# A hybrid conv, pool and MoE layer: norm, router, shared expert and the experts' first weights in one stage with the projection

## The reference

```python
x = x + merged @ w_out                       # output projection and residual: res1
h = rms_norm(x, g_ffn)
scores = sigmoid(h @ w_router)               # 64 experts, 8 groups, best 4 groups, best 8 experts
gates = top_s / sum(top_s) * 2.5
x = x + sum_e gates_e * expert_e(h) + shared(h)      # SwiGLU, 256 wide each
ple_gate = sigmoid(rms_norm(x, g_ple) @ w_ple_gate)
x = x + ple_gate * (p @ w_ple)               # per-layer embedding, p is (1024, 256)
return rms_norm(x, g_final)
```

## Time and profile before

| | us |
|---|---|
| runs (3) | 2092.51, 2092.53, 2095.65; median 2092.53 |
| the profiled execution | 2092.55 |
| its span, first to last instruction | 2090.9 |
| busy: PE, DVE, ACT, POOL | 1855.5, 1378.5, 852.1, 851.6 |
| mean granted TensorE clock | 0.951 of full |

### The profile page before, as it was taken

How to read it: one execution, slowest core, us unless ns; L and a number is a source line. 1 busy time by engine, 2 the same in 40 slices (tenths; PEclk the granted TensorE clock), 3 DMA queues, 4 the chain that set the end, 5 groups by cost and what they waited for, 6 DMA issues and landing times. The chain is left out here.

```text
span 2090.9 us, 32643 instructions
## 1 busy us (share of the span) xinstructions
PE 1855.5 (89%) x8384; PEld 1493.8 (71%) x8385; DVE 1378.5 (66%) x1446; ACT 852.1 (41%) x1000; POOL 851.6 (41%) x688
## 2 busy tenths in 40 slices
PE   4999999988999677859999999999999999993594
PEld 2888888867888356647788778877787777882483
DVE  6299999347651556227666867766777767663766
ACT  4111110145100233246556666766666757561321
POOL 3457777546553220044343333433434434341330
PEclk9999999999999888979999999999999999996797
DMA  2211112212432322279999999999999999975402
GB/s 104 76 50 41 49 60 90 101 68 77 148 115 91 125 101 65 96 279 350 294 280 250 326 315 316 311 290 304 287 285 334 317 302 298 283 208 167 154 30 80
DMA packets 108850, 393.16 MB, mean 188 GB/s; under 512 B 18832, under 2 KB 21008, under 8 KB 100624
## 3 DMA queue, kind: packets, MB, share of 16 engines
q1 hardware_dynamic: 70656, 270.29, 34.9%
q0 software_dynamic: 28944, 88.90, 19.5%
q10 hardware_dynamic: 9216, 33.56, 4.2%
HBM read 329.22 MB, written 83.66 MB: 197 GB/s over the span
## 5 line engine op out<-in xcount | busy, mean ns | idle before, releaser
L168 PE MATMUL bank<-x_hi,w_hi 128*128 128x512 f32 x928 | 366.9, 395 | 26.0 <-DVE x_lo L232 15.9
L169 PE MATMUL bank<-x_lo,w_hi 128*128 128x512 f32 x928 | 364.1, 392 | 0.0
L170 PE MATMUL bank<-x_hi,w_lo 128*128 128x512 f32 x928 | 363.9, 392 | 0.0
L1499 DVE TENSOR_TENSOR gu_lo<-gu_raw,gu_hi 128x1024 fp32r<-128x1024 f32 x260 | 306.9, 1221 | 70.7 <-ACT gu_hi L1426 67.4
L1348 PE MATMUL bank<-gu_hi,xh 128*128 128x512 f32 x776 | 318.5, 410 | 13.6 <-DVE xl L1482 13.6
L1263 POOL DMA_INDIRECT acc_rows<-y,cur x98 | 185.0, 1888 | 352.7 <-ACT y L1422 338.2
L1350 PE MATMUL bank<-gu_lo,xh 128*128 128x512 f32 x776 | 305.7, 394 | 0.0
L1349 PE MATMUL bank<-gu_hi,xl 128*128 128x512 f32 x776 | 303.8, 392 | 0.0
L712 DVE SCALAR_TENSOR_TENSOR bank<-a_buf,c_w_dw,bank 128x1024 f32<-128x1024 f32 x232 | 276.8, 1280 | 0.0
L1426 ACT CAST gu_hi<-gu_raw 128x1024 fp32r<-128x1024 f32 x260 | 260.2, 1052 | 8.5 <-DMA gu_raw<-in_w_gu 8.5
L168 PEld LDWEIGHTS bank<-x_hi,w_hi 128*128 128x128 f32 x928 | 176.3, 190 | 67.7 <-issue 21.8
(11 more groups left out here) (272 smaller groups left out, 2913.3 us busy)
## 6 DMA issues: line engine op xcount, KB each, us to landing
gu_raw<-in_w_gu SPq DMA_DIRECT2D x260, 512.0 KB
dn_raw<-in_w_dn SPq DMA_DIRECT2D x64, 1024.0 KB
w_raw<-in_w_mix SPq DMA_DIRECT2D x56, 512.0 KB, 3.3
acc_in<-acc_rows ACTq DMA_DIRECT2D x16, 512.0 KB, 4.6
acc_rows<-zeros SPq DMA_DIRECT2D x10, 512.0 KB, 9.9
res<-in_x SPq DMA_DIRECT2D x8, 512.0 KB, 7.2
ga_d<-stage ACTq DMA_DIRECT2D x8, 512.0 KB, 2.6
gb_d<-stage ACTq DMA_DIRECT2D x8, 512.0 KB, 2.6
```

The source lines that it names most:

```text
L168: nc.tensor.matmul(o, wh[:, cols], x_hi[:, k, t], start=(i == 0), stop=False)
L169: nc.tensor.matmul(o, wh[:, cols], x_lo[:, k, t], start=False, stop=False)
L170: last = nc.tensor.matmul(o, wl[:, cols], x_hi[:, k, t], start=False, stop=(i == len(ks) - 1))
L1499: nc.vector.tensor_tensor(gl[s][:, w], rg[s][:, w], gh[s][:, w], ALU.subtract).then_inc(gu_split, 1)
```

## The change

Stages 2, 3 and 4 become part of the mixing stage's block; nothing separates them but semaphores.

- The router's weights are scaled by `g_ffn`, and the router product takes the unscaled `res1`. It has a 65th output: `pick` adds the squares of the residual to it, summed over partitions. A call of it (`logits`) stands behind each output chunk, two chunks late. The squares of tiles 0 to 6 are summed on POOL (`run_sq`), those of tile 7 stand by themselves (`part_sq`). The reciprocal root `inv8` is a value per token and is applied where something is evicted: to the logits, to the token rows (`store_rows`, in halves) and, spread to all partitions by a product with a diagonal (`inverse_to_all`), to the shared gate and up products.
- The four shared chunks follow the output chunks. Router, transposes, ranks and lists are called between their steps (`in_first_up`, `in_second_up`, `in_last_up`).
- The lists' one-hot tiles are made by 16 small DVE instructions per tile of tokens; ACT takes no part.
- The shared down products (`shared_down`) are split in their two input tiles; the flip of the first block of tokens stands behind the sixth. The first experts' weights are loaded once the last shared chunk is done. DVE alternates between the sums into `res1` and the low parts of the first expert's weights.
- `res1` goes channel-major to `res_d` and is read back in the last stage, where the rows' copy becomes an addition. Both accumulators start from zeros; 18 blocks are written beside chunks 3 to 11.
- The embedding product moves to the last stage, between the flips of the rows. Its result stays in SBUF.
- The priming scatters of the loop become three short writes to spare rows. Buffers of the loop have new places. The loop's instructions are the same.
- A clear of the semaphores and a barrier stand behind the experts.

The diff, cut to its core:

```diff
@@ sync, mixing stage
-            for n in range(2, END):
+            sp.wait_ge(blank, 1)
+            for n in range(2, ALL):
                 load_chunk(sp, n)
+                if 3 <= n < 3 + NT + 1:
+                    for a in range(2):
+                        sp.dma_start(acc_d[a][(n - 3) * P:(n - 2) * P, :], zeros[:]).then_inc(filled, 16)
...
+            for n in range(NT):
+                sp.wait_ge(evacuated, 2 * n + 2)
+                sp.dma_start(h2_d[n * P:(n + 1) * P, 0:D], rows[:, n % 2]).then_inc(row_out[n % 2], 16)
...
+            sp.wait_ge(done, ALL)
+            for e in range(2):
+                for p, w in enumerate(pieces):
+                    sp.dma_start(rg[e][:, w], i["w_gu"][e][:, w]).then_inc(gu_in[e][p], 16)
...
+            for k in range(KC):
+                sp.wait_ge(sd_read, k + 1)
+                sp.dma_start(res_d[k], res1[:, k, :]).then_inc(res_out[min(k, 2)], 16)
@@ tensor
+            def logits(k):
+                pe.wait_ge(out_read, k + 1)
...
+                for h in range(NH):
+                    t = slice(h * HALF, (h + 1) * HALF)
+                    nc.tensor.matmul(slots[2][0:E + 1, t], wr[:, k, :], res1[:, k, t], start=(k == 0), stop=False)
+            def inverse_to_all():
+                pe.wait_ge(diagonal, 1)
+                for h in range(NH):
+                    t = slice(h * HALF, (h + 1) * HALF)
+                    last = nc.tensor.matmul(slots[3][:, t], ones[:], dg.rearrange("p t e -> p (t e)")[:, t], start=True, stop=True)
+            def list_tokens(n):
+                pe.wait_ge(blocked, n + 1)
+                pe.wait_ge(numbered, n + 1)
...
+            def in_second_up(k):
+                if k == 1:
+                    inverse_to_all()
+                if k in (2, 3, 4):
+                    token_rows(2 * k - 4)
+                    token_rows(2 * k - 3)
+                if k == 5:
+                    ranks()
+                if k == 6:
+                    token_rows(6)
+                    token_rows(7)
+            def in_last_up(k):
+                if k % 2:
+                    list_tokens(k // 2)
...
+            chunk(OUT + 1, y_hi, y_lo)
-            pairs(OUT + 2, END, y_hi, y_lo, out_read, OUT)
+            for ch in range(2, KC):
+                chunk(OUT + ch, y_hi, y_lo)
+                logits(ch - 2)
+            logits(KC - 2)
+            pe.wait_ge(ran, KC - 2)
+            sum_of_squares(run_sq, False)
+            logits(KC - 1)
+            pe.wait_ge(squared2, KC)
+            sum_of_squares(part_sq, True).then_inc(lg_made, 1)
+            chunk(END, x_hi, x_lo, in_first_up)
+            chunk(END + 1, x_hi, x_lo, in_second_up)
+            chunk(END + 2, x_hi, x_lo)
+            chunk(END + 3, x_hi, x_lo, in_last_up)
+            list_tokens(4)
+            list_tokens(5)
+            shared_down(0, 0)
+            list_tokens(6)
+            list_tokens(7)
...
+            for n in range(KC):
+                if n:
+                    shared_down(n, 0)
+                shared_down(n, 1)
+                if n == 5:
+                    pe.wait_ge(gathered[0], 16)
+                    flip_rows(0)
@@ scalar
+            for k in range(KC):
+                act.wait_ge(out_read, k + 1)
+                if k >= 2:
+                    act.wait_ge(ran, k - 1)
+                nc.scalar.activation(part_sq[:] if k else run_sq[:], res1[:, k, :], ACT.Square).then_inc(squared2, 1)
+                nc.scalar.mul(x_hi[:, k, :], res1[:, k, :], g_ffn[:, k:k + 1]).then_inc(h_rounded2, 1)
...
+            def store_rows(n):
+                if n >= 2:
+                    act.wait_ge(row_out[n % 2], 16 * (n // 2))
+                for h in range(NH):
+                    t = slice(h * HALF, (h + 1) * HALF)
+                    act.wait_ge(rows_flipped, 2 * n + h + 1)
+                    nc.scalar.mul(rows[:, n % 2, t], slots[2][:, t], inv8[:, n:n + 1]).then_inc(evacuated, 1)
@@ vector, lists
+            shared_product(0)
             for n in range(NT):
-                v.tensor_tensor(lane_oh[n % 2][:], steps[:, 1:P + 1].unsqueeze(1).to_broadcast([P, TOP_K, P]), mine(lane_of),
-                                ALU.is_equal).then_inc(laned, 1)
-                v.tensor_tensor(block_oh[n % 2][:], steps[:, 0:P].unsqueeze(1).to_broadcast([P, TOP_K, P]), mine(block_of),
-                                ALU.is_equal).then_inc(blocked, 1)
+                for k in range(TOP_K):
+                    at_k = slice(n * TOP_K + k, n * TOP_K + k + 1)
+                    last = v.tensor_scalar(lane_id[n % 2][:, k, :], ramp[:, 1:P + 1], lane_of[:, at_k], token[:, n:n + 1],
+                                           ALU.is_equal, ALU.mult)
+                last.then_inc(numbered, 1)
+                for k in range(TOP_K):
+                    at_k = slice(n * TOP_K + k, n * TOP_K + k + 1)
+                    last = v.tensor_scalar(block_oh[n % 2][:, k, :], ramp[:, 0:P], block_of[:, at_k], None, ALU.is_equal)
+                last.then_inc(blocked, 1)
+                if n == 1:
+                    shared_gate(1)
+                if n == 6:
+                    shared_product(1)
@@ behind the experts
+    sems.clear()
+    nc.all_engine_barrier()
@@ last stage, sync, tensor, scalar, vector
+            for n in range(2):
+                load_rows(n)
+            for k in range(KC):
+                sp.dma_start(res2[:, k, :], res_d[k]).then_inc(res_in, 16)
+            for n in range(2):
+                sp.dma_start(raw[:, n, :], i["w_ple_gate"][n]).then_inc(z.loaded[n], 16)
+            for n in range(2, NT):
+                load_rows(n)
...
+            for n in range(KC):
+                layer_embedding(n)
+                if n % 2:
+                    token_rows(n // 2)
+            for n in range(KC // 2, NT):
+                token_rows(n)
...
+            for k in range(PLE // P):
+                act.dma_start(p_raw[:, k], i["p"][k]).then_inc(ple_in, 16)
+            act.dma_start(ple_raw.rearrange("p (c n) -> p c n", n=PLE), i["w_ple"].rearrange("c p n -> p c n")).then_inc(ple_in, 16)
+            act.wait_ge(ple_in, 16 * (PLE // P + 1))
+            nc.scalar.copy(p_hi[:], p_raw[:]).then_inc(ple_rounded, 1)
+            nc.scalar.copy(ple_hi[:], ple_raw[:]).then_inc(ple_rounded, 1)
...
-                nc.vector.tensor_copy(res2[:, :, n * P:(n + 1) * P], slots[2 + n % 2].rearrange("p (k t) -> p k t", k=KC)
-                                      ).then_inc(back, 1)
+                mine = res2[:, :, n * P:(n + 1) * P]
+                nc.vector.tensor_tensor(mine, slots[2 + n % 2].rearrange("p (k t) -> p k t", k=KC), mine, ALU.add).then_inc(back, 1)
```

More of the change, by code:

```diff
@@ L151, in split_chunk @@
                             ).then_inc(z.split, 1)
-def dense_split(nc, pool, z, count, raw, w_hi, w_lo, cols, first=0):
-    with pool.Fori(first, count // 2) as r:
-        for s in range(2):
-            split_chunk(nc, pool, z, r, 2, s, s, raw, w_hi, w_lo, cols)
 def dense_chunk(nc, ks, wh, wl, x_hi, x_lo, out, before=None):
@@ new lines, in build, with room @@
+    y = [spot("y0", FK + 76, D), spot("y1", FK + 88, D), spot("y2", FK + 92, D)]
+    o8 = [FREE + 96 * KB]
+    def room(name, n, dtype=F32):
+        t = m.at(name, o8[0], [P, n], dtype)
+        o8[0] += (4 * n + 31) // 32 * 32
+        return t
+    xg = [m.at("xg0", XG0, [P, D + GATES], F32)] + [room(f"xg{q}", D + GATES) for q in (1, 2)]
+    gate = [room(f"gate{q}", 1) for q in range(3)]
+    cur = [room(f"cur{q}", 1, I32) for q in range(6)]
+    assert o8[0] <= XG0
+    X_T, Y_P, H_T = slots[0], slots[2], slots[3][:, 0:FF]
@@ new lines, in build @@
+        dn_rounded, dn_split = sem("dn_rounded"), sem("dn_split")
+        gathered = [sem(f"gathered{q}") for q in range(3)]
+        picked, picked_x, picked_y = sem("picked"), sem("picked_x"), sem("picked_y")
+        flipped, x_rounded, x_split = sem("flipped"), sem("x_rounded"), sem("x_split")
+        upped, sigmoided, half, hidden = sem("upped"), sem("sigmoided"), sem("half"), sem("hidden")
+        h_flipped, h_rounded, h_split, downed, y_read = (
+            sem(n) for n in ("h_flipped", "h_rounded", "h_split", "downed", "y_read"))
@@ L406, in _, with further @@
+        def further(b, j):
+            return nc.s_assert_within(b + j, 0, COLS - 2, skip_runtime_bounds_check_because=(
+                "the experts' blocks are at most E + S * TOP_K / P together"))
         @block.sync
@@ L509, in _ @@
                 nc.gpsimd.memset(lev[q][:, 0:UPAD], 0.0).then_inc(padded, 1)
+            nc.gpsimd.memset(zeros[:], 0.0).then_inc(blank, 1)
             pool.wait_ge(padded, 3)
             sums = {30: (1, 2), 31: (3, 4), 32: (5,), 34: (6, 7)}
-            for n in range(2, END):
+            for n in range(2, END + 2):
                 split_weights(pool, n)
@@ L535, in _, with chunk @@
             g_pe = gates[1]
-            def chunk(n, x, l, wait=None):
+            def chunk(n, x, l, between=None):
```

(34 more changed lines are left out.)

1110 lines of the change are left out of this document (532 added, 578 removed).

## The result

| | before | after |
|---|---|---|
| median of 4 runs, us | 2092.52 | 2035.16 (2032.91 to 2038.69) |
| ratio, 95% interval | | 0.9721 (0.9706 to 0.9737) |
| the profiled execution, its span | 2092.55, 2090.9 | 2033.76, 2031.9 |

What follows compares the result with a forecast made beforehand. The prediction took the seam before the expert loop as bound by waiting in turn. 2092.55 - 115.9 (seam) + 25.4 (last stage) + 1.1 (semaphore clear and barrier) = 2003.2 us, range 1988 to 2028.

Steps and rivals of the forecast that it cites:

- the seam: From the last output chunk's end to the experts' first product: 116.0 us in place of 231.9, so -115.9.
- the last stage: Behind the expert loop: rows back 59.6 us after the first transfer in place of 34.2, so +25.4 us.
- the loop: The expert loop, 970.3 us with the same instructions: change 0, bounds -3 and +6 us.
- The router calls between the chunks: Twelve router calls between output chunks, counted in the seam's PE work; four records of 0.43 us per plain call.
- the clear and barrier: Behind the experts: clearing the semaphores and one barrier, +1.1 us.
- joints: Rival: output chunks or first shared products wait 1.4 us at each of 24 joints, 2036.8 us; chance 0.05.
- a loop out of step: Rival: each of the expert loop's 98 blocks waits 1.4 us, 137 us in all, 2140.2 us; chance 0.02.
- a hidden embedding product: Rival: in the last stage transfers bound and the embedding product hides, 1987.2 us; chance 0.12.
- The lists' price: In the seam: DVE's small list instructions at 0.15 us each, 8 x 16 x 0.15 = 19.2 us; bounds 0.13 and 0.35.
- POOL beside DVE: Beside the lists in the seam: POOL's 11.8 us of two-input instructions cost DVE 4.5 us; bounds 0 and 11.8.
- DVE sets the seam's end: Rival: dearer lists and all POOL time bind the seam, 2023.3 us at 0.25 a piece, 2036.1 at 0.35; chance 0.20.
- both are in at t + 12.3: Last stage: embedding inputs and rows, 2.1 MB each, land 12.3 us after its first transfer at 0.41 MB/us.

Runs made afterwards that it cites:

- wide_lists: The lists' 16 small DVE instructions per tile of tokens became two of 128x1024 plus a scaling on ACT, against the changed kernel: 2030.1 us.
- pool_quiet: The changed kernel without POOL's four two-input instructions beside the lists: 2026.7 us.
- h2_act: The gain-scaled residual for the token rows made by ACT in place of POOL, against the changed kernel: 2028.1 us.
- ple_first: In the last stage, residual tiles and gate weights issued only once the embedding inputs have landed, against the changed kernel: 2027.6 us.

## Why the prediction was wrong

The forecast of the profiled execution missed by 30.6 us: 18.9 in the seam, 8.2 in the last stage, 2.7 in the loop, and 0.8 in what is left.

- **Right.** The router calls between the chunks (a chunk takes 12.65 us with one, 1.76 more, where 4 x 0.43 were counted), the shared products, the zero writes at nothing, the hidden gather and weights, the clear and barrier (1.2 for 1.1). The rivals of joints, of a loop out of step and of a hidden embedding product did not come.
- **The lists' price failed**, the 0.15 us apiece. Sixteen instructions take 3.62 us per tile of tokens, 0.23 apiece, where I took 0.15 "as these too run without waits". The row I chose (0.13) was of instructions half as wide, with one input. 8 x (3.62 - 2.4) = 9.8 us; wide_lists took 10.4 off.
- **POOL beside DVE failed.** I priced 4.5 of 11.8 us, on the ground that DVE loses only the rest of an instruction that POOL has begun. But POOL's come in pairs, back to back, and between the two DVE hardly got a turn: it lost 9.8 us, and pool_quiet took 10.1 off the seam. The rule of the Trainium skill, SBUF — State Buffer, "Who interferes with whom", by which whoever starts second is blocked for the whole instruction, gave up to 11.8, and the trace agrees with it better than with my 4.5. Beside POOL's one-input scalings of the residual it doesn't hold (709.62 to 733.32, without a gap): there DVE's two-input row at 721.00 lasted 0.69, as it does alone, and the choice of experts lost 3.5 us in 14.7.
- **A term was missing.** The sum has none for the gain-scaled copy behind the token rows. POOL makes it in 23.7 us for 8 tiles, and PE waited 4.31 us for it. The ranks ended at 53.1 in place of 47.5; h2_act took 6.8 off. The choice of experts, at 19.9 us in place of 14.4, cost nothing, as it ended before the ranks were asked for. 3.3 us more went on the plan behind the ranks, where three of DVE's rows lie beside POOL's (751.51, 755.87 and 757.74), whose time I had priced only from the lists on. So the lists began 9.0 us late.
- These are 9.8 + 5.3 + 9.0 us; 4.0 came back because DVE no longer waited for the fourth product, and 1.2 behind the lists: 18.9. This is the mechanism of the rival "DVE sets the seam's end", which I had at 0.20. It gave 20.1 more for 0.25 apiece and all of POOL's time; that this is near 18.9 is in part luck, for it had no scaled copy in it either.
- **In the last stage** the step "both are in at t + 12.3" failed. I gave the two queues only the 4.2 MB that I looked at, and SP had 5.2 MB more to issue in the same moment. Landing at 20.4 moves the product from 21 to 29.0, the 8 us that are missing, and ple_first gave 7.0 of them back.
- **The loop** stayed within the bounds of -3 and +6, at +2.7.

The range was too narrow because it let these costs go wrong one at a time. All went the same way, and one was not in it.

## What to carry to other kernels

In these kernels a chain of small DVE instructions cost its own time plus nearly all of POOL's two-input time beside it (9.8 us of 11.8, 11.1 of 11.7), so count both engines as one there, and give copies and scalings to ACT if it has room. When a product is moved to a place where its inputs must still be loaded, price the moved load with everything that is issued at that moment, in every queue, and look at what stands behind its first instruction on DVE. When one bound of a stage is taken away, look at the share of the transfers before you expect more. Measure the price of an instruction form at its own width before it is multiplied by 128.

## What the runs showed of the hardware

- A two-input instruction of POOL held up a small one on DVE until its own end: 0.20 us became 4.20 beside 4.59.
- Scaling 128x1024 by a value per partition took POOL 2.84 us a tile, with DVE idle too, where its rounding of the same size with two constants (L309) takes 1.05 and ACT needs 1.06 for the same scaling.
- Eight instructions over 128x128 on DVE take 2.13 us (two operations) or 1.64 (one), one over 128x1024 with two inputs 1.21: per element the small form costs 35 to 75% more.
- An expert loop of the same instructions ran between 970.7 and 977.9 us in kernels that differ only around it, a quarter of a per cent of the whole time and more. With more instructions on DVE ahead of it, it was shorter in all three padded kernels, on one profile each; no cause was shown.
